# Setup behind the fourth key group, a branch output copied before its split, gates moved into the last dilated head, and norm steps at the head of a part

## The reference

```python
h = rms_norm(x, norm_mix)
aq, ak, av, bq, bk, bv, cq = split(h @ w_in)
aq, ak = rms_norm(aq), rms_norm(ak)            # 4 heads x 2 halves of 64 columns
lam = exp(sum(q1 * k1)) - exp(sum(q2 * k2)) + lambda_init
out_a = rms_norm(diff_attention(aq, ak, av, slopes_a, lam), a_subln) * (1 - lambda_init)
bq, bk = rms_norm(bq), rms_norm(bk)            # 3 dilations x 4 heads of 128 columns
out_b = sum_g softmax(lse)_g * dilated_window_attention(bq_g, bk_g, bv_g, ...)
kv = rms_norm(mem, mem_norm) @ w_mem_kv        # 256 memory rows
out_c = memory_attention(rms_norm(cq), rms_norm(ck), cv)
gates = sigmoid(h @ w_gate + b_gate)
x = x + sum(gates * [out_a, out_b, out_c] @ w_branch) @ w_out
x = x + (silu(h2 @ w_ffn_gate) * (h2 @ w_ffn_up)) @ w_ffn_down
```

## Time and profile before

| | |
|---|---|
| median of 3 runs | 3343.69 us (3342.83 to 3343.94) |
| profiled execution, its own time | 3344.81 us |
| its span in the trace | 3342.9 us |
| TensorE busy | 3254.8 us, 97% |
| VectorE busy | 1718.9 us, 51% |
| ScalarE busy | 1119.5 us, 33% |
| weight transfers, share of 16 DMA engines | 26.2% |

### The profile page before, as it was taken

One profiled execution on the slowest core, in us unless ns is written; L12 is line 12 of the kernel. 1 busy time (PEld: TensorE's weight loads), 2 busy tenths in 40 slices (PEclk: granted clock), 3 DMA queues, 4 the chain that ended last, 5 costly groups with the idle time before them and its releaser, 6 DMA issues.

```text
span 3342.9 us, 39813 instructions
## 1 busy us (share of the span) xinstructions
PE 3254.8 (97%) x14944; PEld 2662.5 (80%) x14944; DVE 1718.9 (51%) x2483; ACT 1119.5 (33%) x1771; POOL 0.2 (0%) x4
## 2 busy tenths in 40 slices
PE   9999999999999999999999999999999999999998
PEld 7777777778888888888876888888888878688887
DVE  5664445565443545346754554344543676554542
ACT  4654545532222222232333322232222333332221
POOL 0000000000000000000000000000000000000000
PEclk9999999999999999999999999999999999999999
DMA  4223323232322222331321222322223223122222
GB/s 141 99 78 101 97 74 114 70 114 94 100 94 95 99 95 94 101 111 63 101 95 45 98 97 94 100 95 94 98 97 110 82 76 108 57 89 95 99 95 88
DMA packets 88536, 313.33 MB, mean 94 GB/s; under 512 B 9952, under 2 KB 10336, under 8 KB 87904
## 3 DMA queue, kind: packets, MB, share of 16 engines
q1 hardware_dynamic: 82224, 294.69, 26.2%
q10 hardware_dynamic: 6192, 16.97, 1.6%
HBM read 309.52 MB, written 2.10 MB: 93 GB/s over the span
## 4 chain that ended last, share of the span: by engine, by line
PE 91%; DVE 4%; ACT 3%; issue 2%; DMA 1%; SPq 0%; DVEq 0%; ACTq 0%
PE ps L931 28%; PE ps L933 28%; PE ps L932 27%; PE ps L1201 1%; PE ps L1116 1%; ACT stage_sq L1341 1%; PE ps L1105 1%; PE ps L1148 1%; PE ps L1006 1%; ACT whi L1247 0%; DMA x_res<-in_x 0%; PE ps L1231 0%; PE ps L1094 0%; PE ps L1152 0%; PE ps L1131 0%
## 5 line engine op out<-in xcount | busy, mean ns | idle before, releaser
L931 PE MATMUL ps<-x_hi,whi 128*128 128x512 f32 x2400 | 944.8, 394 | 0.0
L933 PE MATMUL ps<-x_hi,wlo 128*128 128x512 f32 x2400 | 935.5, 390 | 0.0
L932 PE MATMUL ps<-x_lo,whi 128*128 128x512 f32 x2400 | 934.9, 390 | 0.0
L1247 ACT ACTIVATE whi<-raw 128x1024 fp32r<-128x1024 f32 (+1 forms) x555 | 583.2, 1054 | 998.5 <-DMA raw<-in_weights 994.2
L1485 DVE TENSOR_TENSOR wlo<-raw,whi 128x1024 fp32r<-128x1024 f32 x553 | 674.5, 1222 | 418.3 <-ACT whi L1247 409.8
L931 PEld LDWEIGHTS ps<-x_hi,whi 128*128 128x128 f32 x2400 | 451.1, 188 | 97.6 <-issue 5.4
L933 PEld LDWEIGHTS ps<-x_hi,wlo 128*128 128x128 f32 x2400 | 451.0, 188 | 94.6
L932 PEld LDWEIGHTS ps<-x_lo,whi 128*128 128x128 f32 x2400 | 451.1, 188 | 94.3 <-issue 2.4
L933 PE MATMUL ps<-h_hi,wlo 128*128 128x512 f32 x880 | 342.4, 389 | 0.0
L931 PE MATMUL ps<-h_hi,whi 128*128 128x512 f32 x880 | 342.4, 389 | 0.0
L932 PE MATMUL ps<-h_lo,whi 128*128 128x512 f32 x880 | 342.4, 389 | 0.0
(11 more groups left out here) (278 smaller groups left out, 3342.6 us busy)
## 6 DMA issues: line engine op xcount, KB each, us to landing
raw<-in_weights SPq DMA_DIRECT2D x553, 512.0 KB, 3.2
bias<-in_biasB ACTq DMA_DIRECT2D x16, 384.0 KB, 3.2
bias<-in_biasA ACTq DMA_DIRECT2D x16, 256.0 KB, 3.2
mem_raw<-in_mem ACTq DMA_DIRECT2D x3, 1024.0 KB, 7.4
x_res<-in_x SPq DMA_DIRECT2D x8, 256.0 KB, 7.1
x_res<-in_x ACTq DMA_DIRECT2D x1, 2048.0 KB, 9.3
out_x<-x_res SPq DMA_DIRECT2D x8, 256.0 KB, 2.0
raw<-in_weights SPq DMA_DIRECT2D x2, 256.0 KB, 4.4
```

The source lines that it names most:

```text
L931: pe.matmul(out, hi, xhi, start=start, stop=False)
L932: pe.matmul(out, hi, xlo, start=False, stop=False)
L933: return pe.matmul(out, lo, xhi, start=False, stop=stop)
L1247: return act.activation(out, in_, ACT.Copy, scale=scale)
```

## The change

Six edits are made together, all in the first layer's schedule except the third, which also reaches the two cross attentions.

1. `step("setup")` moves from behind the first key part to behind the fourth.
2. The deferred steps of a group: a part flushes at its start and not at its end, and the factors go on a new list, `soon`, that is run at the part's end. So roots and turns stand ahead of a part's matmuls, in the step list one part earlier than before. Turns use both slots only while more than three stand to be done; otherwise each flush does one, into `O`. Where two groups' turns meet (a head's output and a projection group) both go into `O`.
3. `spread` places the first piece of work at its first call and the last at its last call, the others evenly between.
4. The turned output of the first branch is copied (with gain) into `a_stage` by ScalarE, which frees the PSUM slot; ScalarE then copies that to `oa_hi`, and VectorE subtracts from the SBUF copy.
5. The first five gates of the second branch are computed inside that branch's last head, into three further buffers (`GX`); the memory is loaded earlier, and its eight `memfresh` steps stand in two blocks of four behind the first two branch pairs. Gate 5 stands between the keys and the values of the memory.
6. Turned tiles of the memory attention alternate between `T0` and `T1`. In the second branch the second score bank is freed by the copy of the far blocks alone.

```diff
@@ part of group(), and the deferred steps @@
         def part(u):
+            self.flush()
             unit = len(self.units)
...
-            self.flush()
+            self.flush_soon()
...
         def roots():
             self.step("ginv", **a)
-            self.defer(factors)
+            self.soon.append(factors)
...
         def turns():
-            for slot in ("O", "T0") if isinstance(a["g"], tuple) else ("T0", "O"):
-                if turned:
-                    self.step("gturn", c=turned.pop(0), slot=slot, **a)
+            for slot in ("O", "T0")[:2 if len(turned) > 3 else 1]:
+                self.step("gturn", c=turned.pop(0), slot=slot, **a)
             if turned:
                 self.defer(turns)
         self.defer(roots)
+
+    def flush_soon(self):
+        soon, self.soon = self.soon, []
+        for go in soon:
+            go()
@@ spread @@
+    places = [1 + round(k * (slots - 1) / max(len(work) - 1, 1)) for k in range(len(work))]
...
-        upto = len(work) * min(state[1], slots) // slots
-        while state[0] < upto:
+        while state[0] < len(work) and places[state[0]] <= state[1]:
@@ build_schedule @@
     step("consts")
-    step("setup")
...
     a_keys[3]()
+    step("setup")
     step("masks")
...
+    GATE_B = [("GT", 0), ("GT", 1), ("GX", 0), ("GX", 1), ("GX", 2), ("GT", 0), ("GT", 1), ("GX", 0)]
...
+    b_work = [b_parts[12:20], b_parts[20:28], b_parts[28:37],
+              b_parts[37:38] + [memload] + b_parts[38:] + [lambda m=m: gate_b(m) for m in range(5)]]
...
+    for jj in range(2):
+        pair_b(jj)
+        for go in memparts[4 * jj:4 * jj + 4]:
+            go()
     memsum()
-    gate_b(5)
...
-    for go in c_keys + c_values:
+    for go in c_keys + [lambda: gate_b(5)] + c_values:
         go()
@@ TensorE @@
-                    free[a["slot"]] = (("olo", role["id"]) if role["dst"][0] == "OA" else
-                                       ("hgated", a["g"][1:]) if role["dst"][0] == "MIX" else ("hq", role["id"]))
+                    free[a["slot"]] = (("hgated", a["g"][1:]) if role["dst"][0] == "MIX" else ("hq", role["id"]))
...
-                    wait_free("T0", "S1") if a["kind"] == "B" else wait_free("T0")
+                    wait_free(turn_slot(a), "S1") if a["kind"] == "B" else wait_free(turn_slot(a))
...
-                        free["S1"] = ("pt", i)
+                        free["S1"] = ("pt", (i, "far"))
@@ ScalarE @@
                     if role["dst"][0] == "OA":
-                        copy(OAH[:, role["dst"][1], :], src, gain_of(role["gain"])).then_inc(*sig("ohi", role["id"]))
+                        whole = AOS[role["dst"][1] % 2].rearrange("p t c d -> p (t c d)")
+                        copy(whole, src, gain_of(role["gain"])).then_inc(*sig("hq", role["id"]))
+                        act.wait_ge(*on("hq", role["id"]))
+                        copy(OAH[:, role["dst"][1], :], whole).then_inc(*sig("ohi", role["id"]))
```

More of the change, by code:

```diff
@@ L85, in __init__ @@
         self.later = []
+        self.soon = []
         self.inverses = []
@@ L195, in drain @@
     def drain(self):
-        while self.later:
+        while self.later or self.soon:
             self.flush()
+            self.flush_soon()
     def settle(self):
@@ L396, in build_schedule, with memory, gate_b @@
         branch_pair(0, "OA", lambda m: ("Y", m), jj)
-    b_work = [b_parts[12:20], b_parts[20:28], b_parts[28:37], b_parts[37:] + [lambda m=m: gate_chunk(1, m, ("GT", m)) for m in range(2)]]
+    def memory(n, which, gain):
+        return ([lambda: step("memload", n=n, which=which, after=("evac", s.njobs - 1) if n else ("olo", ("B", NHEAD - 2)))]
+                + [lambda m=m: step("memfresh", n=n, m=m, gain=gain) for m in range(DC)]
+                + [lambda: s.norms.extend([("rstdm", n)] * (n > 0) + [("rstdmc", n)])])
+    GATE_B = [("GT", 0), ("GT", 1), ("GX", 0), ("GX", 1), ("GX", 2), ("GT", 0), ("GT", 1), ("GX", 0)]
+    def gate_b(m):
+        gate_chunk(1, m, GATE_B[m])
+    memload, *memparts, memsum = memory(0, 0, "mem_norm")
+    b_work = [b_parts[12:20], b_parts[20:28], b_parts[28:37],
+              b_parts[37:38] + [memload] + b_parts[38:] + [lambda m=m: gate_b(m) for m in range(5)]]
     for h in range(NHEAD):
         attend(b_tiles[h], b_work[h])
[L401 to L408, removed]
-    def pair_b(jj):
[L411 to L419, removed]
+    def pair_b(jj):
+        branch_pair(1, "OB", lambda m: GATE_B[m], jj)
+    for jj in range(2):
+        pair_b(jj)
+        for go in memparts[4 * jj:4 * jj + 4]:
+            go()
     memsum()
-    gate_b(5)
     c_keys = s.group("w_mem_kv", 0, [h for h in heads], [turned(("CK", h), "c_k_norm", ("CK", h), P) for h in heads],
@@ L874, in program, with turn_slot, turned_in @@
         TURN = {"T0": PS[:, 2, :], "O": O}
+        def turn_slot(a):
+            return "T1" if a["kind"] == "C" and a["i"] % 2 else "T0"
+        def turned_in(a):
+            return PS[:, 3 if turn_slot(a) == "T1" else 2, :]
         def probs(a):
@@ L1624, in _ @@
                     dve.wait_ge(*on("ohi", role["id"]))
-                    dve.scalar_tensor_tensor(OAL[:, role["dst"][1], :], TURN[a["slot"]], gain_of(role["gain"]),
-                                             OAH[:, role["dst"][1], :].bitcast(F32), ALU.mult, ALU.subtract)\
-                        .then_inc(*sig("olo", role["id"]))
+                    dve.tensor_tensor(OAL[:, role["dst"][1], :], AOS[role["dst"][1] % 2].rearrange("p t c d -> p (t c d)"),
+                                      OAH[:, role["dst"][1], :].bitcast(F32), ALU.subtract).then_inc(*sig("olo", role["id"]))
                 elif kind == "rstdm":
```

12 lines of the change are left out of this document (7 added, 5 removed).

## The result

The changed kernel takes 3362.59 us (median of 4 runs, 3361.0 to 3364.25) against 3343.26 us for the kernel before in the same conditions (4 runs, 3340.25 to 3343.94): a ratio of 1.0057, 95% interval 1.0045 to 1.007. It is 19 us slower. The forecast was 3360, the range 3338 to 3371.

What follows compares the result with a forecast made beforehand. TensorE, busy for 97% of the span, was taken to bound the kernel by its matmuls plus gaps. Terms summed to +18.6 us, less 2.6 by choice, +16: 3360.8 profiled, forecast 3360 us, range 3338 to 3371.

Steps and rivals of the forecast that it cites:

- Setup behind the keys: After the fourth key part: TensorE's lambda sum waits for VectorE's queued work, +5.3 us; first key turns behind it, +1.5.
- Opening: Start of the kernel: moving setup removes TensorE's 4.29 us wait but not the constants' load behind it, -1.6 us.
- Query turns: Turns of the queries: TensorE reaches them one part earlier, before the factors are done, +2.1 us.
- First branch: First branch with gates: turns a part earlier wait for copies and maxima, 21.0 us replacing 9.2, so +11.9.
- Dilated heads 0 to 2: Dilated branch, first three heads: turns a part earlier, waits of 9.65 us against 6.25, so +3.4.
- Last dilated head: Last head of the dilated branch: five gate jobs and spread pieces fill its waits, -7.2 us.
- Memory sum: Sum over memory chunks: VectorE needs 17.2 us after the second product against TensorE's 13.7, so +3.5.
- Memory attention: Memory attention: two slots for turned tiles and longer work between tiles cut gaps from 5.6 to about 3.0, -2.6 us.
- Rest of the program: Cross attentions: only the places of work change, +0.5 us, bounds -1 to +4.
- Clock: Lower TensorE clock beside waits, more numerous in keys and first branch: one more stretch net, +2 us.
- clock rival: Each wait of about 2 us or more brings a low-clock stretch: 10 us in place of 2, 3368; chance 0.15.
- faster rival: VectorE and ScalarE get ahead during TensorE's first new wait, so first-branch turns find slots free: 3332 us; chance 0.12.

Runs made afterwards that it cites:

- experiment 1: Changed kernel with the setup step put back behind the first key part: 3356.6 us, ratio 1.0041 to the kernel before.
- experiment 9: The changed kernel measured again with no edit: 3359.58 us, ratio 1.0048 to the kernel before.
- experiments 3 to 5 and 10: Changed kernel with first-branch output turned into T0 (3353.2 us), old spread places (3359.64), one output copy (3357.32); kernel before with only setup moved (3349.55).
- Experiment 2: Changed kernel with the old order of deferred steps, turns in pairs to T0 and O: 3339.88 us, ratio 0.9992 to the kernel before.
- experiment 3: Changed kernel with the first branch's head output turned into T0 instead of O: 3353.2 us, ratio 1.0033 to the kernel before.

## Why the prediction was right, point by point

The direction and the size (+16 forecast, +19.3 and +15.8 measured) hold, and the signs that were named for it came: the wait of 5 us at the lambda sum, those on the two turns in slot `O`, 19.3 us of gaps in the first branch, 1.98 and 3.97 in the last dilated head and in the memory attention. Not all terms hold.

- **Setup behind the keys** (+5.3, +1.5 behind it): the wait was 5.00 us, as worked out. The +1.5 did not come; the rows in experiment 1 show that 0.6 to 0.8 of it was left, and that the lower clock took this up.
- **Opening** (-1.6): its wait fell from 4.29 to 2.67, released by the transfer, as the earlier trace rows let one expect. But TensorE is through with the fourth key part at 36.6 us for 39.2 before, which is 2.6 earlier, at 36.3 in the trace of experiment 9 and between 34.2 and 34.7 in those of experiments 3 to 5 and 10: the term was too small, and it moves by 2 us from one execution to the next.
- **Query turns** (+2.1): 1.72. The prediction reads the turns as 1.44 behind the end of the second factor; by the earlier trace rows that is the end of the fourth (69.87 + 2.86), and the second ends at 71.3. The sum does not rest on it.
- **First branch** (21.0 of waits in place of 9.2): 19.3. One by one: 3.7 forecast, 3.74 measured; 3.6, 3.38; 5.5, 5.20; 2.95, 2.57. From its own rows the prediction should have had 5.3 - 1.9 = 3.4 for the second and 4.8 for the third; why it took 3.6 and 5.5 it does not say. Experiment 2 shows that the order and slots of the deferred steps make these waits, experiment 3 that the double use of `O` is one half of it.
- **Dilated heads 0 to 2** (9.65 of waits in place of 6.25): 7.5, with the largest at 3.63.
- **Last dilated head** (-7.2): the gaps fell by 5.2 to 2.0.
- **Memory sum** (+3.5): 1.24 + 2.09 = 3.3. **Memory attention** (-2.6): from its first score on the gaps are 4.0 for 7.5, -3.5.
- **Rest of the program** (+0.5 for the cross attentions): from the memory attention's end on, the gaps are 46.5 for 48.1, -1.6.
- **Clock** (+2): this is the term that was mis-sized. TensorE's busy time grew by 9.5 us over the program. In the first layer, where the change is, it grew by 10.3 (sum of the six windows, 636.8, against 626.5 before), and by 9.8 in the trace of experiment 9. (Over the whole program that trace has 6.3, since the later layers, which hardly change, had less of the lower level in it.) In the first trace the new waits of 5.00, 3.74, 3.38, 5.20 and 3.63 all have the lower level at them; in that of experiment 9 the 3.38 has not, and those of 2.57 and 2.33 have. The clock rival's price of 10 was right for the first layer, and which wait gets the lower level is not fixed.
- **What makes up for it:** the terms without the clock come to +16.6, or to +14.0 with the 2.6 taken off by choice, for which no row was given. The gaps grew by 8.6. The 8.0 that are missing from 16.6 stand in the opening with keys and queries (+4.2 for +7.3), the first branch (+10.2 for +11.9), the dilated heads 0 to 2 (+1.2 for +3.4), the rest of the program (-1.6 for +0.5) and the memory attention (0.9), less 2.0 in the last dilated head.

So the gaps were put 5.4 us too high and the clock 7.5 too low, and that the sum is so near is the luck of their balance. The mechanism of the waits is shown; their sum and the clock's share were each missed by more than the forecast as a whole, which lies 2.6 below the first measurement and 0.4 above the second.

The faster rival would have needed VectorE to reach the product's copy less than 2 us after the product's end. The product ends at about 176.0 and the copy starts at 180.35, 4.4 after. (The 5.2 that the prediction reads from the earlier trace rows is the copy's end; its start is 4.5 after.) The lower end of the range, 3338, is given as the case in which the terms of first branch and memory fail, but 3360 - 11.9 - 3.5 is 3344.6.

By the Trainium skill (ScalarE: Activation LUTs, What ACT_TABLE_LOAD costs) a switch of the table set takes 2.66 us in all. The trace of the changed kernel has this switch between a copy and an exponential:

```profile
182.27 0.57 ACT L1262 ACTIVATE probs_t<-ps 128x512 f32<-128x512 f32 x1
...
182.86 1.28 ACT L1417 ACT_TABLE_LOAD   x1
...
184.16 0.72 ACT L1417 ACTIVATE probs<-probs,small 128x512 f32<-128x512 f32 x1
```

From the end of the copy (182.84) to the exponential are 1.32 us, so the measurement decides for the 1.28 that the prediction used: none of the 1.38 that the page adds as a drain shows here.

## What to carry to other kernels

With in-order queues, moving a step earlier is safe only where what it reads and the slot it writes are ready at the new place on every engine; the durations and queue contents around one neighbouring instance gave five of the new waits (5.00, 3.74, 3.38, 5.20, 2.57) to 0.4 us in the first trace. Two uses of one buffer with nothing between them cost the latency of its reader's whole queue, not of its copy. A change of order has to be priced twice, as the wait and as the lower clock around it: in the first layer the second was here as large as the gaps (about 10 us each). Waits in one chain should not be added, since the first wait and the slower matmuls behind it give the next one's producer time. Edits bundled together should be split: here one part lost some 20 us and another won 5, and a combination that leaves the first out is 12 us faster than the kernel before.

## What the runs showed that I had not expected

The time at the lower clock differs between runs at one and the same wait. In the second layer, which the change does not touch at this place, a wait of 2.64 us ends at 1682.37 before, and one of 2.65 at 1700.42 after:

```profile
1682.30:1689.10 6.80, 6.73 (x19) 5.47 (x20) 4.15 (x6) 1.58 (x2) 0.00 (x0) 0.55 0.03 11
```

```profile
1700.40:1703.80 3.40, 3.38 (x11) 2.92 (x12) 2.60 (x4) 1.15 (x2) 0.00 (x0) 0.57 0.05 19
1703.80:1707.20 3.40, 3.40 (x16) 2.79 (x16) 1.50 (x2) 0.43 (x1) 0.00 (x0) 1.00 0.00 0
```

Before, 6.8 us at about half speed (19 matmuls); after, 3.4 us and then full speed (11 and 16 matmuls). That is a difference of 1.7 us from a single wait (half of 3.4). The kernel before has 8 stretches at the lower level in its whole trace and the changed one 14, and such differences may be a part of why medians of the same kernel lie up to 3 us apart. The opening is another: with the same schedule it differs by 2.3 us between traces (experiment 1).
